# Expert down projection: every other pair of tiles 32 to 119 as seven block products, with sums of blocks on GpSimd

## The chip, the cores and the metric

The kernel runs on one core of one Trainium2 chip. The metric is the device time in microseconds. The profiles name the engines PE (TensorE), PEld (its weight loads), DVE (VectorE), ACT (ScalarE), POOL (GpSimd) and SP (SyncE, which here only issues transfers).

## The reference

Two transformer blocks over 256 tokens of 1024 features, all in float32. The first has two layers, each with a mixer, a feed-forward part with product-key experts, and a gated per-layer embedding. The change is in the last sum of the experts, once for each layer:

```python
def expert_block(args):          # peer_ffn; K = 16 experts for each of 8 heads, of 16384
    xb, eb, gb = args
    ub = jnp.take(u, eb, axis=0)
    act = jax.nn.gelu(jnp.einsum('thkd,td->thk', ub, xb), approximate=False)
    vb = jnp.take(v, eb, axis=0)
    return jnp.einsum('thk,thkd->td', gb * act, vb)
...
x = layer_norm(DN_ALPHA * x + peer_ffn(x, ...), ln_g[i, 1], ln_b[i, 1])
x = x + jax.nn.sigmoid(x @ ple_w_gate[i]) * (p[i] @ ple_w_proj[i])
```

## The kernel before

It gathers no experts. All 16384 are computed for all tokens, as 128 tiles of 128 experts: stage u turns each tile of `u` into a block of gelus [128 experts x 256 tokens], with a gate of zero where a token didn't choose the expert, and these 128 blocks fill `big`. Stage v multiplies block j (as weights of TensorE, in two halves of 128 tokens) with tile j of `v` [128 experts x 1024 features], and adds all 128 into four PSUM banks, `acc`: two token halves by two feature halves of 512. Then the layer norm follows, from `acc` and X.

Each float32 product is made of three in the fp32r type: high x high, low x high and high x low. For a tile of v ScalarE casts the high part from the ring (`take_high`, L433), VectorE subtracts for the low part (`take_low`, L445), and the same two do this for the block of gelus (`stage`, L1574 and L2255, into `x_parts`). TensorE's `split_wide` (L826) then has 3 parts x 2 token halves x 2 feature halves, 12 matmuls of 512 columns. In stage u and in the first tile of most other stages GpSimd makes the low parts (also L445); in stage v it has nothing to do.

The order is written out by hand, one instruction stream for each engine. SP loads tiles into a ring of four (`tile_landed`), each when the low part of the tile four before is done. `w_hi` and `w_lo` have two buffers each: ScalarE casts tile j + 1 once TensorE has begun tile j (`tiles_begun`). `stage(j + 2)` stands behind `take_high(j + 1)`. On all engines the stage is a loop over bodies of eight tiles. Behind the last tile TensorE transposes, runs fillers on zeros (L875) to fill the wait, and takes up the next weight matrix when the layer norm on VectorE, ScalarE and GpSimd is through.

## Time and profile before

| | us |
|---|---|
| median of 3 runs | 2625.51 (2624.88 to 2627.14) |
| profiled execution, its own time | 2623.45 |
| its span, first to last instruction | 2621.7 |
| PE busy | 2583.5 (99%) |
| PEld busy | 2214.6 (84%) |
| DVE busy | 1743.4 (67%) |
| ACT busy | 1495.7 (57%) |
| POOL busy | 670.6 (26%), nearly all of it in the two u stages |

The times of single instructions come from the one profiled execution. A busy TensorE isn't one at its peak, since matmuls are pipelined; how long a tile takes is read from the starts of its matmuls. The idle time of an engine costs nothing by itself: what counts is which wait ends last.

### The profile page before, as it was taken

To read this page: it belongs to the slowest core of one execution; us is meant where nothing else is said; L and a number is where in the kernel's file an instruction comes from. 1 tells how busy PE (TensorE), PEld (TensorE's weight loads), DVE (VectorE), ACT (ScalarE), POOL (GpSimd) and SP (SyncE) were. 2 spreads that over 40 slices of the span, in tenths; PEclk is the share of its full clock that TensorE was granted. 3 is DMA by queue.
4 is the path that set the end of the run, shared out by engine and by line. 5 is a ranking of instruction groups with operands and counts; after the bars stand their busy time and mean duration, and the time that the engine had idled before them with its cause. 6 is when DMAs were issued, how large, how long until landed. Compare 5 with 4: busy or idle time off the path is not lost.

```text
span 2621.7 us, 43906 instructions
## 1 busy us (share of the span) xinstructions
PE 2583.5 (99%) x15010; PEld 2214.6 (84%) x15010; DVE 1743.4 (67%) x3219; ACT 1495.7 (57%) x2852; POOL 670.6 (26%) x310
## 2 busy tenths in 40 slices
PE   8999999999999999999999999999999999999998
PEld 7789988887888887789988887888888887877887
DVE  4568778886555565459778885555567746555774
ACT  4445488885445554444588884444555545564553
POOL 0007877672000000018877671000001000001000
PEclk9999999999999999999999999999999999999999
DMA  6345544445555544345544446555556565535564
GB/s 223 89 160 177 185 156 159 153 156 200 193 192 192 192 162 148 109 153 185 177 156 159 153 162 200 194 193 193 192 169 197 191 194 170 161 111 161 168 192 153
DMA packets 124331, 447.66 MB, mean 171 GB/s; under 512 B 14312, under 2 KB 14952, under 8 KB 123936
## 3 DMA queue, kind: packets, MB, share of 16 engines
q1 hardware_dynamic: 120096, 434.16, 51.0%
q0 software_dynamic: 2608, 9.08, 1.2%
q10 hardware_dynamic: 1488, 2.59, 0.3%
q8 instruction: 83, 1.36, 0.2%
q14 instruction: 56, 0.46, 0.1%
HBM read 444.74 MB, written 1.05 MB: 170 GB/s over the span
## 4 chain that ended last, share of the span: by engine, by line
PE 94%; DVE 2%; ACT 2%; DMA 1%; issue 1%; ACTq 0%; POOL 0%; DVEq 0%
PE ps L826 41%; PE ps L782 21%; PE ps L787 10%; PE ps L798 4%; PE ps L804 4%; PE ps L801 4%; PE ps L1046 3%; PE ps L1118 1%; PE ps L1015 1%; ACT w_hi L433 0%; PE ps L733 0%; DMA ring<-in_v 0%; PE ps L1064 0%; PE ps L887 0%; DVE stats L1937 0%
## 5 line engine op out<-in xcount | busy, mean ns | idle before, releaser
L433 ACT CAST w_hi<-ring 128x1024 fp32r<-128x1024 f32 (+1 forms) x812 | 852.1, 1050 | 765.3 <-PE ps L826 521.2
L445 POOL TENSOR_TENSOR w_lo<-ring,w_hi 128x1024 fp32r<-128x1024 f32 x267 | 641.4, 2403 | 1679.3 <-ACT w_hi L433 1480.7
L445 DVE TENSOR_TENSOR w_lo<-ring,w_hi 128x1024 fp32r<-128x1024 f32 x545 | 664.8, 1220 | 549.8 <-ACT w_hi L433 540.0
L826 PE MATMUL ps<-w_hi,x_parts 128*128 128x512 f32 x2976 | 743.9, 390 | 4.7 <-ACT w_hi L433 3.2
L826 PEld LDWEIGHTS ps<-w_hi,x_parts 128*128 128x128 f32 x2976 | 553.0, 188 | 125.7 <-issue 8.9
L782 PE MATMUL ps<-x_parts,w_hi 128*128 128x512 f32 x2320 | 591.9, 397 | 0.1
L782 PEld LDWEIGHTS ps<-x_parts,w_hi 128*128 128x128 f32 x2320 | 416.0, 189 | 75.5 <-ACT w_hi L433 0.3
L826 PE MATMUL ps<-w_lo,x_parts 128*128 128x512 f32 x1488 | 402.2, 388 | 0.3 <-DVE w_lo L445 0.3
L787 PEld LDWEIGHTS ps<-x_parts,w_lo 128*128 128x128 f32 x2320 | 316.5, 190 | 22.6
L826 PEld LDWEIGHTS ps<-w_lo,x_parts 128*128 128x128 f32 x1488 | 277.8, 188 | 59.4 <-DVE w_lo L445 1.6
L787 PE MATMUL ps<-x_parts,w_lo 128*128 128x256 f32 x2320 | 323.0, 282 | 0.0
L798 PE MATMUL ps<-x_parts,w_hi 128*128 128x256 f32 x784 | 192.8, 284 | 0.0
L801 PE MATMUL ps<-x_parts,w_hi 128*128 128x256 f32 x784 | 192.3, 283 | 0.0
L1394 ACT COPY tops<-ps 128x256 f32<-128x256 f32 x294 | 106.7, 363 | 141.1 <-PE ps L787 137.4
L1542 ACT ACTIVATE SC<-SC 128x128 bf16<-128x128 bf16 x512 | 163.6, 392 | 8.8 <-DVE SC L2207 8.7
L2213 DVE TENSOR_TENSOR SC<-SC,ps 128x512 bf16<-128x512 bf16 x256 | 164.4, 683 | 4.4
L2207 DVE TENSOR_TENSOR SC<-iota,ps 128x1024 bf16<-128x1024 f32 x128 | 154.8, 1209 | 0.1
L798 PEld LDWEIGHTS ps<-x_parts,w_hi 128*128 128x128 f32 x784 | 150.4, 192 | 0.6 <-issue 0.4
L801 PEld LDWEIGHTS ps<-x_parts,w_hi 128*128 128x128 f32 x784 | 150.5, 192 | 0.0
L804 PE MATMUL ps<-x_parts,w_lo 128*128 128x256 f32 x784 | 110.0, 283 | 0.0
L1046 PE MATMUL ps<-SC 128*128 128x128 bf16 x1536 | 108.0, 220 | 0.0
L2255 DVE TENSOR_TENSOR x_parts<-big,x_parts 128x256 fp32r<-128x256 f32 x256 | 106.7, 417 | 0.2
(287 smaller groups left out, 2196.8 us busy)
## 6 DMA issues: line engine op xcount, KB each, us to landing
ring<-in_u SPq DMA_DIRECT2D x256, 512.0 KB, 3.5
ring<-in_v SPq DMA_DIRECT2D x256, 512.0 KB, 4.2
ring<-in_ffn_in SPq DMA_DIRECT2D x88, 512.0 KB, 3.8
ring<-in_ffn_out SPq DMA_DIRECT2D x44, 512.0 KB, 4.2
ring<-in_wq SPq DMA_DIRECT2D x32, 512.0 KB, 3.4
ring<-in_ple_gate SPq DMA_DIRECT2D x16, 512.0 KB, 3.7
SC<-in_rows POOLq DMA_DIRECT2D x11, 512.0 KB, 5.0
ring<-in_a_qk SPq DMA_DIRECT2D x8, 512.0 KB, 4.9
```

What stands on the lines that cost most here:

```text
L433: nc.scalar.copy(part(w_hi, i)[:, used(name)], tile(i)[:, used(name)]).then_inc(tiles_hi, 1)
L445: eng.tensor_tensor(part(w_lo, i)[:, at], tile(i)[:, at], part(w_hi, i)[:, at], ALU.subtract).then_inc(tiles_low[LOW[n][0]], 1)
L782: mm = nc.tensor.matmul(both, hi[:, k, :], x_parts[:, :, k, :], start=(k == 0), stop=False)
L787: mm = nc.tensor.matmul(bank(s)[:, 0:T], lo[:, k, :], x_hi[:, k, :], start=False, stop=(k == KC - 1))
L798: mm = nc.tensor.matmul(bank(s)[:, 0:T], hi[:, k, :], x_hi[:, k, :], start=(k == 0), stop=False)
L801: nc.tensor.matmul(bank(s)[:, 0:T], hi[:, k, :], x_lo[:, k, :], start=False, stop=False)
L804: mm = nc.tensor.matmul(bank(s)[:, 0:T], lo[:, k, :], x_hi[:, k, :], start=False, stop=(k == KC - 1))
L826: mm = nc.tensor.matmul(acc[:, 2 * tb + f, 0:cnt], x[:, k + c, tb * P:(tb + 1) * P], part(w, i)[:, at:at + cnt], start=(first and n == 0 a ...
L1046: mm = nc.tensor.matmul(bank(s)[:, t * P:(t + 1) * P], one_hots[:, n % 2, 1, t], gated_rows[:, n % 2, piece, t], start=(piece == 0), stop= ...
L1542: ins = S.mul(gated_rows[:, n % 2, 2, t], one_hots[:, n % 2, 0, t], gate_low[:, at:at + 1])
L2207: V.tensor_tensor(one_hots[:, n % 2], iota[:, None, None, :].to_broadcast([P, 2, GROUP, P]), chosen[:, :, :, None].to_broadcast([P, 2, GRO ...
L2213: V.tensor_tensor(gated_rows[:, n % 2, piece], one_hots[:, n % 2, 0], part_of[:, :, None].to_broadcast([P, GROUP, P]), ALU.mult).then_inc( ...
```

## The change

In tiles 32 to 119 a body of eight has two mixed pairs, tiles 0 and 1 and tiles 4 and 5 of it, and two pairs of plain tiles as before. A mixed pair is a 2 x 2 block product: rows are the two token halves, columns the two feature halves, and the inner index is the tile of the pair. It is done with seven block products in place of eight (Strassen's scheme in Winograd's form). Three add into `acc` as before. Four add into the banks 4 to 7, over all pairs of the layer, and are folded into X at the end.

What comes with it: GpSimd makes three sums of v's blocks, one more in place, and the low part of the three (`block_sums_of`). ScalarE casts the high part of the sums (`sums_high`). VectorE makes four sums of the gelu blocks (`rows_mixed`) and their low parts (`rows_low`), and ScalarE their high parts. Two blocks of gelus are staged by one instruction (`stage_pair`). Tiles 4 and 5 of a body land in a buffer of their own in `big`, so a pair can stay longer. At the end ScalarE copies the four banks, multiplies X by DN_ALPHA, and GpSimd's `fold` adds them in seven instructions; the layer norm then has the weight 1.0. `ple_side` moves from `big` to `SC` and is copied eight tiles before the mixed ones.

```diff
+            def block_sums_of(layer):                      # GpSimd
+                pool.wait_ge(staged, EXPERT_TILES * layer + 26)
+                def pair(m, b, turns):
...
+                    b21, b22 = tile(i)[:, 0:512], tile(i)[:, 512:D]
+                    b11, b12 = tile(i + 1)[:, 0:512], tile(i + 1)[:, 512:D]
+                    if b or m:
+                        pool.wait_ge(sums_low, turns * MIX_PAIRS + p)
+                    G.tensor_tensor(block_sums[:, 0], b11, b12, ALU.add).then_inc(pair_sums, 1)
+                    made(1)
+                    G.tensor_tensor(block_sums[:, 1], block_sums[:, 0], b22, ALU.add).then_inc(pair_sums, 1)
+                    made(2)
+                    G.tensor_tensor(block_sums[:, 2], block_sums[:, 1], b21, ALU.add).then_inc(pair_sums, 1)
+                    G.tensor_tensor(b12, b12, b22, ALU.add).then_inc(pair_sums, 1)
+                    pool.wait_ge(sums_hi, turns * MIX_PAIRS + (p + 1))
+                    G.tensor_tensor(sum_lo[:], block_sums[:], sum_hi[:], ALU.subtract).then_inc(sums_low, 1)
...
+            def fold(layer):                               # GpSimd, 7 instructions, 4096 elements
+                pool.wait_ge(mix_moved, 5 * layer + 5)
+                G.tensor_tensor(V, m6, m1, ALU.subtract).then_inc(mix_folded, 1)
...
+                def mixed_pair(m, b, turns=0, first=False, last=False):      # TensorE
...
+                    pe.wait_ge(staged, turns * BODY + (EXPERT_TILES * layer + j + 2))
+                    pe.wait_ge(mixed_low, turns * MIX_PAIRS + (p + 1))
+                    def products(group, low, apart):
+                        for n in range(3):
+                            if n == 2 and low:
+                                low()
+                            for dst, x, w in group:
+                                mm = nc.tensor.matmul(dst, x[n % 2], w[n // 2], ...)
+                    own = [ps[:, 4 + n, :] for n in range(4)]
+                    mm = products([(c11, raw(k, one), halves_of(i, left)), (c12, row(3), halves_of(i, right))],
+                                  lambda: lo_here(name, j, turns), lambda dst: False)
+                    begins_tile(mm)
+                    pe.wait_ge(sums_low, turns * MIX_PAIRS + (p + 1))
+                    mm = products([(c21, raw(k, two), sums(2)), (own[1], row(0), sums(0)), (own[2], row(2), sums(1))],
+                                  None, lambda dst: dst is not c21)
+                    begins_tile(mm)
+                    hi_here(name, j + 1, turns)
+                    mm = products([(own[0], raw(k + 1, one), halves_of(i + 1, left)),
+                                   (own[3], row(1), halves_of(i + 1, right))],
+                                  lambda: lo_here(name, j + 1, turns), lambda dst: True)
+                    mm.then_inc(sums_used, 1)
...
+                def sums_high(m, b, turns=0):              # ScalarE
+                    act.wait_ge(pair_sums, turns * (4 * MIX_PAIRS) + (4 * p + 3))
+                    if b or m:
+                        act.wait_ge(sums_used, turns * MIX_PAIRS + p)
+                    S.copy(sum_hi[:], block_sums[:]).then_inc(sums_hi, 1)
+                def mixed_half(s, b, turns=0, last=False):
+                    take_high(act, name, at + s + 1, turns)
+                    stage_pair(at + s + 4, turns)
+                    take_high(act, name, at + s + 2, turns)
+                    if ahead:
+                        sums_high(*where)
+                    take_high(act, name, at + s + 3, turns)
+                    if ahead:
+                        rows_high(*where)
+                    take_high(act, name, at + s + 4, turns)
+                    stage_pair(at + s + 6, turns)
...
+                def mixed_half(s, b, turns=0, last=False): # VectorE
+                    if ahead:
+                        rows_mixed(*where)
+                    take_low(dve, name, at + s + 1, turns)
+                    stage_pair(at + s + 4, turns)
+                    take_low(dve, name, at + s + 2, turns)
+                    take_low(dve, name, at + s + 3, turns)
+                    if ahead:
+                        rows_low(*where)
+                    take_low(dve, name, at + s + 4, turns)
+                    stage_pair(at + s + 6, turns)
...
-                layer_norm(f"v{layer}", f"ln{layer}_1")
+                dve.wait_ge(mix_folded, 7 * (layer + 1))
+                layer_norm(f"v{layer}", f"ln{layer}_1", 1.0)
```

VectorE's loop of the v stage before, from its top, two of the eight tiles (L445 is `take_low`, L2255 is `stage`; REGISTER_ALU and ISA are the loop's arithmetic and waits):

```order
L2260 UNCONDITIONAL_BRANCH
L2260 ISA
L445 TENSOR_TENSOR w_lo<-ring,w_hi 128x1024
L2254 REGISTER_ALU
L2255 ISA
L2255 TENSOR_TENSOR x_parts<-big,x_parts 128x256
L443 REGISTER_ALU
L445 TENSOR_TENSOR w_lo<-ring,w_hi 128x1024
```

The same engine now, in the loop over tiles 32 to 111, the first half of a body without its last two instructions (`big` is also where the row sums and the tiles of the second pair are; L2605 to L2610 is `rows_mixed`, L2616 `rows_low`, L2590 `stage_pair`, L502 `take_low`):

```order
L2605 TENSOR_TENSOR big<-big 128x256
L2601 ISA
L2608 TENSOR_TENSOR big<-big 128x128
L2601 REGISTER_ALU
L2610 ISA
L2610 TENSOR_TENSOR big<-big 128x128
L500 ISA
L502 TENSOR_TENSOR w_lo<-ring,w_hi 128x1024
L2589 REGISTER_ALU
L2590 TENSOR_TENSOR x_parts<-big,x_parts 128x512
L500 REGISTER_ALU
L502 TENSOR_TENSOR w_lo<-ring,w_hi 128x1024
```

Four tiles have ten such instructions on VectorE in place of eight. GpSimd before, between the last low part of stage u and the layer norm's scaling (L445 here is the low part of the next stage's first tile, L669 `scale_first`):

```order
L445 TENSOR_TENSOR w_lo<-ring,w_hi 128x1024 x7
L641 DMA SC<-in_rows 128x1024 x2
L445 TENSOR_TENSOR w_lo<-ring,w_hi 128x1024
L669 TENSOR_TENSOR X<-X,SC 128x512 x2
```

And now, at the same place: the first pair, then (from L813 with `big<-big` on) the second, whose tiles are in `big`:

```order
L773 DMA SC<-in_rows 128x1024 x2
L813 TENSOR_TENSOR big<-ring 128x512
L815 TENSOR_TENSOR big<-big,ring 128x512
L817 TENSOR_TENSOR big<-big,ring 128x512
L818 TENSOR_TENSOR ring<-ring 128x512
L820 TENSOR_TENSOR sum_lo<-big,sum_hi 128x1536
L813 TENSOR_TENSOR big<-big 128x512
L815 TENSOR_TENSOR big<-big 128x512
L817 TENSOR_TENSOR big<-big 128x512
L818 TENSOR_TENSOR big<-big 128x512
L820 TENSOR_TENSOR sum_lo<-big,sum_hi 128x1536
```

A loop with 20 further pairs and the fold follow, all of which read and write SBUF alone.

## Rows read from the trace of the kernel before

**Rows 1.** section 1 of the page, each engine's busy us, share and instructions:

```profile
PE 2583.5 (99%) x15010; PEld 2214.6 (84%) x15010; DVE 1743.4 (67%) x3219; ACT 1495.7 (57%) x2852; POOL 670.6 (26%) x310
```

**Rows 2.** chain that ended last, 600 to 975, start, us, what:

```profile
625.42 341.65 PE ps L826 x1506
967.10 1.23 DVE X L1927
```

**Rows 3.** stretches of both v stages, busy us of each engine (instructions), clock, DMA:

```profile
core 0: us, PE busy (x) PEld busy (x) DVE busy (x) ACT busy (x) POOL busy (x), PEclk, DMA share, GB/s
625.00:967.00 342.00, 341.58 (x1507) 282.87 (x1508) 196.20 (x251) 172.81 (x256) 0.00 (x0) 1.00 0.59 194
1597.00:1937.00 340.00, 340.00 (x1502) 281.52 (x1501) 194.54 (x250) 171.08 (x253) 0.01 (x1) 1.00 0.59 193
```

**Rows 4.** timeline of PE, 955 to 975, start, us, line, operation:

```profile
957.38 1.98 PE L826 MATMUL ps<-w_hi,x_parts 128*128 128x512 f32 x8
...
960.10 1.98 PE L826 MATMUL ps<-w_hi,x_parts 128*128 128x512 f32 x8
...
971.71 1.89 PE L875 MATMUL ps<-zeros 128*128 128x512 bf16 x8
```

**Rows 5.** groups by line, 630 to 950: count, busy us, mean ns, idle:

```profile
L826 PE MATMUL ps<-w_hi,x_parts 128*128 128x512 f32 x942 | 232.8, 389 | 0.0
L445 DVE TENSOR_TENSOR w_lo<-ring,w_hi 128x1024 fp32r<-128x1024 f32 x118 | 144.5, 1225 | 137.0 <-ACT w_hi L433 137.0
L2255 DVE TENSOR_TENSOR x_parts<-big,x_parts 128x256 fp32r<-128x256 f32 x118 | 49.2, 417 | 0.0
L433 ACT CAST w_hi<-ring 128x1024 fp32r<-128x1024 f32 x118 | 124.5, 1055 | 160.9 <-PE ps L826 160.9
L1574 ACT CAST x_parts<-big 128x256 fp32r x118 | 47.6, 403 | 0.0
```

**Rows 6.** waits, 620 to 950: us in total, times, longest:

```profile
ACT w_hi L433 <- PE ps L826: 165.4, 121, 2.8
DVE w_lo L445 <- ACT w_hi L433: 143.7, 120, 3.4
```

**Rows 7.** groups by line, GpSimd, whole span:

```profile
L445 POOL TENSOR_TENSOR w_lo<-ring,w_hi 128x1024 fp32r<-128x1024 f32 x267 | 641.4, 2403 | 1679.3 <-ACT w_hi L433 1480.7 <-DVEq L1833 198.3
L669 POOL TENSOR_TENSOR X<-X,SC 128x512 f32<-128x512 f32 x8 | 10.1, 1270 | 8.2 <-ACT X L1341 8.2
```

**Rows 8.** timeline of DVE and POOL, at 325 and from 602 to 611:

```profile
325.70 0.43 DVE L1814 TENSOR_TENSOR SC<-SC 128x256 f32<-128x256 f32 x1
325.76 2.63 POOL L445 TENSOR_TENSOR w_lo<-ring,w_hi 128x1024 fp32r<-128x1024 f32 x1 [1.15 <-ACT w_hi L433]
...
602.53 2.40 POOL L445 TENSOR_TENSOR w_lo<-ring,w_hi 128x1024 fp32r<-128x1024 f32 x1 [1.13 <-ACT w_hi L433]
...
603.14 0.67 DVE L2223 TENSOR_TENSOR big<-big,ps 128x496 f32<-128x496 f32 x1 [1.88 <-ACT big L1532]
...
605.37 2.41 POOL L445 TENSOR_TENSOR w_lo<-ring,w_hi 128x1024 fp32r<-128x1024 f32 x1 [0.43 <-ACT w_hi L433]
...
605.68 2.38 DVE L2236 TENSOR_TENSOR big<-SC,big 128x256 f32<-128x256 f32 x1 [0.88 <-ACTq L1525]
...
608.16 2.41 POOL L445 TENSOR_TENSOR w_lo<-ring,w_hi 128x1024 fp32r<-128x1024 f32 x1 [0.38 <-ACT w_hi L433]
...
608.92 1.92 DVE L2236 TENSOR_TENSOR big<-SC,big 128x256 f32<-128x256 f32 x1 [0.53 <-ACTq L1525]
```

**Rows 9.** groups by line, VectorE, whole span, L2236 with both operands in SBUF:

```profile
L2236 DVE TENSOR_TENSOR big<-SC,big 128x256 f32<-128x256 f32 x8 | 10.3, 1288 | 4.9 <-ACTq L1525 4.9
```

**Rows 10.** timeline of DVE, the start of the layer norm:

```profile
967.10 1.22 DVE L1927 SCALAR_TENSOR_TENSOR X<-X,ps 128x1024 f32<-128x1024 f32 x1 [1.49 <-PE ps L826]
```

**Rows 11.** section 6 of the page, issue to landing:

```profile
ring<-in_v SPq DMA_DIRECT2D x256, 512.0 KB, 4.2
```

**Rows 12.** stretch where PE is idle most after a v stage:

```profile
972.00:976.00 4.00, 2.64 (x17) 1.71 (x16) 3.32 (x10) 1.15 (x4) 1.50 (x2) 1.00 0.06 23
```

More of the change, by code:

```diff
@@ L430, in take_high @@
             i = TILE[name] + j
[L431 removed]
+            tile_here(act, i, turns)
             part_free(act, i, turns)
@@ L687, in _ @@
                 load_rows(2 * layer + 1, (tiles_gated, tiles_with_gates(layer, EXPERT_TILES - 1)))
+                block_sums_of(layer)
+                fold(layer)
                 take_low(pool, f"ple_gate{layer}", 0)
@@ L1076, in peer, with mixed_body @@
+                def mixed_body(b, turns=0, first=False, last=False):
+                    for s in (0, 4):
+                        if s in MIX_AT:
+                            mixed_pair(MIX_AT.index(s), b, turns, first, last and s == MIX_AT[-1])
+                        for j in range(s + 2 if s in MIX_AT else s, s + 4):
+                            down(MIX_FROM + BODY * b + j, turns)
+                        first = first and MIX_AT[0] > s
                 for j in range(BODY):
                     down(j)
-                with pe.Fori(1, EXPERT_TILES // BODY - 1, 1) as turns:
+                with pe.Fori(1, MIX_FROM // BODY, 1) as turns:
@@ L1079, in peer @@
                     for j in range(BODY, 2 * BODY):
                         down(j, turns - 1)
-                for j in range(EXPERT_TILES - BODY, EXPERT_TILES):
+                moved(pe, SLOT[f"ple_proj{layer}"], 4)
+                mixed_body(0, first=True)
+                with pe.Fori(1, MIX_BODIES - 1, 1) as turns:
+                    mixed_body(1, turns - 1)
+                mixed_body(MIX_BODIES - 1, last=True)
+                for j in range(MIX_TO, EXPERT_TILES):
                     down(j)
+                pe.wait_ge(mix_moved, 5 * layer + 4)
@@ new lines, in mixed_half @@
+                def mixed_half(s, b, turns=0, last=False):
+                    at, name = MIX_FROM + BODY * b, f"v{layer}"
+                    n = (s + 4) % BODY
+                    ahead = n in MIX_AT and not last
+                    where = (MIX_AT.index(n), b + (s + 4) // BODY, turns) if ahead else None
+                    if s in MIX_AT:
+                        third_sum(at + s + 1, b, turns)
+                    take_high(act, name, at + s + 1, turns)
[8 more added lines that the diff above has]
+                    stage_pair(at + s + 6, turns)
@@ new lines, in rows_low @@
+                def rows_low(m, b, turns=0):
+                    p = pairs_before(layer, b, m)
+                    dve.wait_ge(mixed_hi, turns * MIX_PAIRS + (p + 1))
+                    V.tensor_tensor(row_lo[:], row_sums[:], row_hi[:], ALU.subtract).then_inc(mixed_low, 1)
+                def mixed_half(s, b, turns=0, last=False):
+                    at, name = MIX_FROM + BODY * b, f"v{layer}"
+                    n = (s + 4) % BODY
+                    ahead = n in MIX_AT and not last
+                    where = (MIX_AT.index(n), b + (s + 4) // BODY, turns) if ahead else None
+                    if ahead:
[8 more added lines that the diff above has]
+                    stage_pair(at + s + 6, turns)
```

266 lines of the change are left out of this document (245 added, 21 removed).

## The prediction, made before the changed kernel ran

> **What bounds the kernel now.** I read the engines' shares first, then the chain that ended last, then the stage that is changed, and last every place where GpSimd and VectorE work at once. TensorE is busy for 99% of the span [rows 1]; the reader should take from it that all other engines have slack on average, GpSimd most. The chain of waits says the same of the changed stage: one unbroken piece of 341.65 us of L826 matmuls, from 625.42 on, and then VectorE's layer norm [rows 2]. Both layers have the stage, with 1508 and 1502 matmuls in 342 and 340 us, at a granted clock of 1.00, with VectorE at 57% and GpSimd at zero [rows 3]. In the timeline a tile takes 2.72 us, 12 matmuls of 512 columns, so 0.2267 us each [rows 4]; four tiles take 10.88. VectorE does 1.225 + 0.417 us in a tile and ScalarE 1.055 + 0.403 [rows 5], and each waits for the engine ahead of it, ScalarE 165.4 us for TensorE and VectorE 143.7 us for ScalarE in 330 us [rows 6]. So today TensorE is the bound, and a matmul removed there is worth 0.2267 us as long as nothing else grows beyond it.
>
> **What it removes.** 88 tiles of a layer (32 to 119) become 22 mixed pairs and 22 pairs of plain tiles. A pair was 24 matmuls and is now 7 products of 3 parts, 21. Their width stays 512 and each has its own weight load as before. Four tiles (one mixed pair, two plain tiles: a half body) go from 48 matmuls to 45: 10.20 us in place of 10.88, and 44 times 0.68 is 29.9 us in the two layers. That is all that can be won.
>
> **What it adds, for four tiles.** On GpSimd, where nothing ran: four tensor_tensor of 512 elements and one of 1536. Rows give 2.40 us for 1024 and 1.27 for 512 [rows 7], so 2.21 ns an element and 0.14 us fixed; the five are 4 x 1.27 + 3.53 = 8.61 us, of which 3584 x 2.21 ns = 7.92 is the work on elements. On VectorE: four low parts of 1024 (as before), two stagings of 512 in place of four of 256, and for the row sums 256, 128, 128 and then 512: 6144 elements. By 1.225 for 1024 and 0.417 for 256 [rows 5] it is 1.05 ns an element and 0.15 fixed: 6.45 us on elements, and with the ten fixed parts 7.9. ScalarE gets two casts of 512, 0.62 each, for four of 256, a cast of 1536 (1.49) and one more of 512: 4.2 + 1.2 + 1.5 + 0.6 = 7.5 us. Taken one engine at a time all of this lies beside 10.2 us of matmuls and costs nothing.
>
> **Where the cover is gone.** The engines cannot be taken one at a time. At 605.68 VectorE begins a tensor_tensor of 256 elements from SC and big, both in SBUF. It ought to take 0.42 us and takes 2.38, while GpSimd's own subtraction runs from 605.37 to 607.78; VectorE's ends at 608.06, 0.28 us after, which is the 0.27 that 256 elements need. The next pair of rows repeats it: 1.92 us, ending 0.27 after GpSimd's. It goes the other way too: GpSimd's at 325.76 takes 2.63 us and ends 2.26 after VectorE's two-SBUF-operand instruction, which is 1024 elements of 2.21 ns. An instruction of VectorE with one operand in PSUM, at 603.14, lies wholly inside GpSimd's 602.53 to 604.93 and takes its usual 0.67 [rows 8]. So two SBUF operands on VectorE and a tensor_tensor on GpSimd exclude each other for the whole instruction, in either order, with only the fixed part hidden. In the kernel before this costs next to nothing, since in the stages where GpSimd splits tiles VectorE mostly reads PSUM. In the changed stage every instruction of both engines has only SBUF operands.
>
> The Trainium skill (SBUF — State Buffer, "Who interferes with whom") says the same of two SBUF inputs and a GpSimd instruction that reads SBUF, and calls it an exclusive lock for the whole instruction. The rows agree, though each shows one instruction held up, none both engines queued without a break. By that rule the two engines' work adds up, as it does below; were the port shared without loss, the 10.2 us of the matmuls would stand.
>
> The floor for four tiles is then 7.92 + 6.45 = 14.4 us. The ceiling is all durations end to end, 8.6 + 7.9 = 16.5, with about 1 us in which both wait for someone else: 17.5. Both lie above 10.2. To choose I lay one half body out, from t = 0 where TensorE ends the mixed pair. ScalarE's cast of 1536 waits for that and ends at 1.55. GpSimd's 1536 then holds the port from 1.63 to 5.16. The low part of the second plain tile has its high part at 2.6 and must wait: it ends at 6.24, where TensorE wanted it at 4.53, and TensorE is through with that tile at 7.2 in place of 5.4. From 5.2 on GpSimd's four 512s (1.13 each) and VectorE's low rows 0.54, low part 1.08, staging 0.54 take turns: 13.0. The row sums, three with a wait of each other, bring 13.95, the next low part 15.1, and two last matmuls end the pair at 15.6. TensorE waits in four pieces of 0.8 to 1.8 us. I take 15.6; the order of the turns moves it by 0.6 down or 1 up. There are 21 such half bodies in a layer, since the last prepares no pair and only gains 0.68: 21 x (15.6 - 10.88) - 0.7 = 98.4 us a layer, 196.9 for both. At the floor it is 21 x 3.5 - 0.7 = 73 a layer, at the ceiling 138.
>
> **The way in and out.** For the first pair GpSimd begins once tile 26 is staged, with some 16 us ahead, and its 7.9 us beside four tiles of VectorE's fit. I take 1 us a layer, between 0 and 3. At the end ScalarE copies four banks and scales X beside tiles 121 to 124: a cast (1.05), a copy of 512 (0.59) and 2048 elements (1.92) behind the start of tile 123, so the fold on GpSimd begins about 1.0 us after tile 124 does. Its seven instructions hold 4096 elements, 9.05 us, with some 1.1 of fixed parts and waits in a chain, and VectorE's three last low parts take 3 x 1.08 of the port: 14.4 after the start of tile 124. VectorE waits for it ahead of the layer norm, which before began 9.7 us after that tile's start (967.10 against 957.38) [rows 4, 10]. The layer norm is wholly on the path there, TensorE has only a transposition and fillers beside it. So 5 us a layer, between 1 and 8. The bank copies moved, ple_side's new place and the 10 more semaphores I take at nothing: ScalarE has 3 us to spare in four tiles. Transfers too: a tile lands in 4.2 us [rows 11], its number is unchanged, and pair tiles are asked for eight ahead. If that cover went, a half body that waits for a landing would cost what is left of it, within the ceiling.
>
> **Sum.** Profiled execution before 2623.45; + 196.9 + 2 + 10 = 2832.4. The median of the runs shown is 2.06 over the profiled one, so 2834 us.
>
> **Rivals.**
> A, the other side, not slower: the port is not held when both queues are full (or the two long stalls were something else), and everything added hides behind TensorE. Then 2623.45 - 29.9 + 2 + 10 = 2605.6, and 2607.6 by the median. For it: the engines' shares, and that such stalls are rare: L2236 has eight instructions with both operands in SBUF, at a mean of 1288 ns against some 420 [rows 9]. Against it: stretches that end to 0.01 us with the other engine's instruction, both ways, in both layers. It decides if the union of both engines' work comes below 10.2 us in four tiles. 5%.
> B: TensorE's idle pieces, a third of the stage, cost it its clock. A matmul at the lower level of 1.2 GHz would take up to twice as long, 45 x 0.453 = 20.4 us for four tiles, TensorE bound again: 21 x 9.5 = 200 a layer, 3037 us if it held all through. Against it: in the slice of before where TensorE is idle most, 972 to 976 with 2.64 of 4 us busy, the granted clock is 1.00 [rows 12]; no row here has it at the lower level. The Trainium skill (TensorE: Matmul & The Clock Gate, Part 1) has the clock depend on how busy the engine has been lately; by it part of the stage could fall, by the row none. 5%.
> C: the turns go badly. If VectorE always loses to GpSimd's four 512s, or the 1536 waits behind the low parts and the pair waits for it, a half body passes the ceiling, at 18.5 say: 21 x 7.6 x 2 = 320, 2956 us. For it: the sum_lo, the low part and the row sums are each on the way to TensorE, with one buffer each. 7%.
> D: the lock is there, but VectorE's short instructions slip in unseen, so that a half body is 12 to 14 us: around 2725. Nothing in the rows speaks for it. 4%.
>
> **How the numbers follow.** The forecast has 79%. Its own range runs from the floor, 2625.5 + 146 + 2, to the ceiling, 2625.5 + 276 + 22: 2774 to 2924. I give 2772 to 2930; that leaves out A, B, most of C and D, and little of the forecast. A measurement of this kernel tells about 0.2%, 5 us. Faster: A and a bit of doubt, 0.06; within 0.2%: 0.01; slower: 0.93.
>
> **What would show it.** Right: in the changed stage TensorE at about 65% busy, four tiles every 15 to 16 us, waits of L1299 and the plain tiles' matmuls for VectorE's low parts, low parts of 1024 that last up to 4.6 us where GpSimd's 1536 lies beside them, GpSimd's 512s stretched from 1.27 towards 2.3, a clock still at 1.00, and a layer norm that waits for GpSimd. Wrong: VectorE's low parts at 1.22 throughout and four tiles in 10.2 (A); a stage clock near half (B); TensorE waiting mostly for landings.

## The result, and the profile after

| | before | after |
|---|---|---|
| median, us | 2626.26 (4 runs, 2624.88 to 2627.14) | 2837.77 (4 runs, 2837.3 to 2840.0) |
| profiled execution's own time | 2623.45 | 2840.0 |
| its span | 2621.7 | 2837.3 |

The ratio is 1.0808, with an interval of 1.0794 to 1.0823: 211.5 us slower, where 2834 us and a range of 2772 to 2930 were predicted. The span grew by 215.6 us.

Section 1 and three groups of section 5 of the page of after (busy us, mean ns of one, idle time before):

```profile
PE 2637.0 (93%) x14869; PEld 2212.5 (78%) x14878; DVE 2100.4 (74%) x3301; ACT 1579.8 (56%) x2856; POOL 1190.8 (42%) x544
...
L502 DVE TENSOR_TENSOR w_lo<-ring,w_hi 128x1024 fp32r<-128x1024 f32 (+1 forms) x501 | 688.8, 1379 | 383.4 <-ACT w_hi L490 372.9
...
L820 POOL TENSOR_TENSOR sum_lo<-big,sum_hi 128x1536 fp32r<-128x1536 f32 x44 | 171.4, 3895 | 94.9 <-ACT sum_hi L1847 94.9
...
L2590 DVE TENSOR_TENSOR x_parts<-big,x_parts 128x512 fp32r<-128x512 f32 x94 | 183.7, 1955 | 0.0
```

By the code TensorE has 132 matmuls fewer, 3 for each of 44 pairs, and the weight loads show just that (15010 and 14878; nine matmul records are missing from the trace). Its busy share falls from 99% [rows 1] to 93%. VectorE's staging of 512 elements, 0.69 us by the prediction's figures (512 x 1.05 ns and 0.15), lasts 1.96 in the mean, and GpSimd's low part of 1536, 3.53 by them, lasts 3.90. The windows of after answer to [rows 3]; this one is the inside of both changed stages:

```profile
750.00:1020.00 270.00, 211.52 (x813) 156.48 (x812) 261.43 (x180) 129.45 (x144) 205.42 (x90) 0.95 0.41 139
1830.00:2080.00 250.00, 196.00 (x751) 144.59 (x749) 242.44 (x167) 120.01 (x134) 188.35 (x82) 0.95 0.42 140
```

VectorE is busy for 261.43 of 270 us. Nearly half of that is waiting inside instructions, since an instruction that is held up counts as busy: 270 us hold 17.8 times four tiles, and by the prediction's 7.9 us each VectorE's own work is 141 us. Without the other engine's rows this looks like an engine at its limit. The groups of 750 to 1030 show it against [rows 5] and [rows 7]:

```profile
L502 DVE TENSOR_TENSOR w_lo<-ring,w_hi 128x1024 fp32r<-128x1024 f32 x57 | 101.3, 1790 | 3.9 <-ACT w_hi L490 3.9
L1019 PE MATMUL ps<-w_hi,x_parts 128*128 128x512 f32 x293 | 80.8, 421 | 0.0
L2590 DVE TENSOR_TENSOR x_parts<-big,x_parts 128x512 fp32r<-128x512 f32 x38 | 79.7, 2097 | 0.0
L820 POOL TENSOR_TENSOR sum_lo<-big,sum_hi 128x1536 fp32r<-128x1536 f32 x18 | 71.7, 3983 | 41.9 <-ACT sum_hi L1847 41.9
...
L813 POOL TENSOR_TENSOR big<-big 128x512 f32<-128x512 f32 x9 | 18.8, 2087 | 8.2 <-DMA big<-in_v 7.5 <-POOL sum_lo L820 0.7
```

The low part takes 1790 ns where it took 1225, and GpSimd's first sum 2087 where such an instruction took 1270. The waits of the same stretch (us in total, times, longest) say who paid:

```profile
PE ps L1019 <- DVE w_lo L502: 31.9, 18, 2.5
PE ps L1299 <- DVE w_lo L502: 24.1, 29, 1.3
```

Then half a body in the timeline of after (start, us; in brackets the idle time before and what ended it):

```profile
802.50 4.38 POOL L820 TENSOR_TENSOR sum_lo<-big,sum_hi 128x1536 fp32r<-128x1536 f32 x1 [2.90 <-ACT sum_hi L1847]
...
803.91 4.05 DVE L502 TENSOR_TENSOR w_lo<-ring,w_hi 128x1024 fp32r<-128x1024 f32 x1 [0.40 <-ACT w_hi L490]
...
807.05 2.06 POOL L813 TENSOR_TENSOR big<-big 128x512 f32<-128x512 f32 x1 [0.17 <-POOL sum_lo L820]
807.89 1.77 DVE L2616 TENSOR_TENSOR row_lo<-big,row_hi 128x512 fp32r<-128x512 f32 x1
808.02 1.19 PE L1019 MATMUL ps<-w_lo,x_parts 128*128 128x512 f32 x4 [0.91 <-DVE w_lo L502]
...
809.71 0.50 PE L1299 MATMUL ps<-w_hi,x_parts 128*128 128x512 f32 x1 [0.50 <-DVE row_lo L2616]
...
811.94 0.50 PE L1299 MATMUL ps<-w_lo,x_parts 128*128 128x512 f32 x1 [1.04 <-DVE w_lo L502]
...
816.97 0.50 PE L1299 MATMUL ps<-w_lo,x_parts 128*128 128x512 f32 x1 [1.33 <-DVE w_lo L502]
```

The low part of 803.91 ends at 807.96, 1.08 us behind GpSimd's end at 806.88, and 1.08 is what its 1024 elements need. GpSimd's sum ends at 809.11 and VectorE's row_lo 0.55 later, which is 512 elements. TensorE waits 0.91 + 0.50 + 1.04 + 1.33 = 3.78 us in this half body. A body takes 30.27 us (for example 802.56 to 832.83), or 15.13 for four tiles, against 10.88 before. TensorE needs 10.20 of them at full clock.

The other half of this body has one longer wait, and a stretch in which TensorE runs slower. The two halves as windows, and lines of TensorE in the second:

```profile
802.56:817.70 15.14, 11.36 (x46) 8.14 (x46) 14.56 (x10) 7.23 (x8) 13.00 (x6) 1.00 0.37 139
817.70:832.83 15.13, 12.42 (x46) 9.46 (x46) 14.77 (x12) 7.14 (x8) 10.01 (x6) 0.89 0.42 139
```

```profile
822.01 1.41 PE L1019 MATMUL ps<-w_lo,x_parts 128*128 128x512 f32 x4 [2.46 <-DVE w_lo L502]
823.22 3.40 PE L1019 MATMUL ps<-w_hi,x_parts 128*128 128x512 f32 x8
```

One instruction of VectorE, the first row sum (`rows_mixed`), in three half bodies in a row:

```profile
798.36 1.51 DVE L2605 TENSOR_TENSOR big<-big 128x256 f32 x1
...
813.50 1.51 DVE L2605 TENSOR_TENSOR big<-big 128x256 f32 x1
...
828.63 1.51 DVE L2605 TENSOR_TENSOR big<-big 128x256 f32 x1
```

In the first half the granted clock is 1.00, in the second 0.89, where eight matmuls last 3.40 us in place of 1.98, and still both take 15.1 us (TensorE's first plain matmuls behind a pair start at 802.40, 817.54 and 832.66). VectorE's instruction comes every 15.10 to 15.15 us from 738 to 1025, while TensorE begins its pairs 12.6 to 17.7 us apart. So the pace of the stage is that of VectorE and GpSimd taking turns, and a slower TensorE only fills some of its own waits.

**The ledger.** Landmarks of the two traces (starts of the same tiles), us added:

| | predicted, a layer | layer 0 | layer 1 |
|---|---|---|---|
| way in (start of tile 30 to first pair, less 5.44) | 1 | 7.6 | 8.3 |
| 22 half bodies (239.4 before) | 98.4 | 329.1 - 239.4 = 89.7 | 332.4 - 239.4 = 93.0 |
| fold: start of tile 124 to layer norm (9.72 before) | 5 | 14.03 - 9.72 = 4.3 | 4.3 |
| behind the layer norm's start (to tile 30 of layer 1; to the end) | 0 | 3.3 | 2.7 |

They sum to 213.3. The other 2.4 us of the span's 215.6 lie ahead of tile 30 of layer 0, nearly all within the first 140 us, where both kernels do the same.

### The profile page after: what moved, and what is told of

Same layout as the page of the kernel before. It is cut to its first block, busy times and chain, and to the rows that moved or that the text cites. A ratio compares the mean times of both kernels' runs of the same rounds, so it can differ in the third digit from the quotient of the medians.

```text
span 2837.3 us, 44061 instructions
## 1 busy us (share of the span) xinstructions
PE 2637.0 (93%) x14869; PEld 2212.5 (78%) x14878; DVE 2100.4 (74%) x3301; ACT 1579.8 (56%) x2856; POOL 1190.8 (42%) x544
## 3 DMA queue, kind: packets, MB, share of 16 engines
HBM read 444.74 MB, written 1.05 MB: 157 GB/s over the span
## 4 chain that ended last, share of the span: by engine, by line
PE 73%; DVE 14%; issue 6%; ACT 3%; POOL 2%; DMA 1%; DVEq 1%; ACTq 0%; SPq 0%; POOLq 0%
PE ps L1019 23%; PE ps L975 19%; PE ps L980 10%; DVE x_parts L2590 4%; DVE w_lo L502 3%; PE ps L991 3%; PE ps L997 3%; PE ps L994 3%; PE ps L1239 3%; DVE big L2605 2%; DVE row_lo L2616 2%; PE ps L1299 1%; ACT w_hi L490 1%; DMA ring<-in_v 1%; PE ps L1376 1%
## 5 line engine op out<-in xcount | busy, mean ns | idle before, releaser
L490 ACT CAST w_hi<-ring 128x1024 fp32r<-128x1024 f32 x768 | 804.9, 1048 | 699.9 <-PE ps L1019 377.6
L502 POOL TENSOR_TENSOR w_lo<-ring,w_hi 128x1024 fp32r<-128x1024 f32 x267 | 641.3, 2402 | 983.4 <-ACT w_hi L490 784.8
L502 DVE TENSOR_TENSOR w_lo<-ring,w_hi 128x1024 fp32r<-128x1024 f32 (+1 forms) x501 | 688.8, 1379 | 383.4 <-ACT w_hi L490 372.9
L1019 PE MATMUL ps<-w_hi,x_parts 128*128 128x512 f32 x2272 | 597.3, 404 | 23.6 <-ACT w_hi L490 21.1
L1019 PEld LDWEIGHTS ps<-w_hi,x_parts 128*128 128x128 f32 x2272 | 438.5, 196 | 126.7 <-issue 17.3
L1019 PE MATMUL ps<-w_lo,x_parts 128*128 128x512 f32 x1136 | 323.0, 402 | 72.5 <-DVE w_lo L502 72.2
L980 PE MATMUL ps<-x_parts,w_lo 128*128 128x256 f32 x2320 | 323.0, 282 | 0.0
L1019 PEld LDWEIGHTS ps<-w_lo,x_parts 128*128 128x128 f32 x1136 | 214.2, 193 | 137.2 <-DVE w_lo L502 94.0
L820 POOL TENSOR_TENSOR sum_lo<-big,sum_hi 128x1536 fp32r<-128x1536 f32 x44 | 171.4, 3895 | 94.9 <-ACT sum_hi L1847 94.9
L2590 DVE TENSOR_TENSOR x_parts<-big,x_parts 128x512 fp32r<-128x512 f32 x94 | 183.7, 1955 | 0.0
L813 POOL TENSOR_TENSOR big<-ring 128x512 f32<-128x512 f32 x22 | 44.4, 2017 | 190.6 <-DMA ring<-in_v 189.8
```

The lines of the kernel that those rows point to most:

```text
L490: nc.scalar.copy(part(w_hi, i)[:, used(name)], tile(i)[:, used(name)]).then_inc(tiles_hi, 1)
L502: eng.tensor_tensor(part(w_lo, i)[:, at], tile(i)[:, at], part(w_hi, i)[:, at], ALU.subtract).then_inc(tiles_low[LOW[n][0]], 1)
L820: G.tensor_tensor(sum_lo[:], block_sums[:], sum_hi[:], ALU.subtract).then_inc(sums_low, 1)
L980: mm = nc.tensor.matmul(bank(s)[:, 0:T], lo[:, k, :], x_hi[:, k, :], start=False, stop=(k == KC - 1))
L1019: mm = nc.tensor.matmul(acc[:, 2 * tb + f, 0:cnt], x[:, k + c, tb * P:(tb + 1) * P], part(w, i)[:, at:at + cnt], start=(first and n == 0 a ...
L2590: V.tensor_tensor(x_lo[:, j % BODY:j % BODY + 2, :].rearrange("p a b -> p (a b)"), pair_rows(j, turns), x_hi[:, j % BODY:j % BODY + 2, :]. ...
```

## The experiments

In what follows "the port" is what VectorE, with two SBUF operands, and a GpSimd that reads SBUF cannot use at once; the traces show the turns, not the wiring. "The kernel before" ran beside each, with medians of 2625.0 to 2626.3. The first two, and two later ones, put work on GpSimd beside the unchanged stage of before. Where a range is given a kernel ran four times (one_pair_spread eleven times), where it isn't, once. Ahead of tile 30 of layer 0, where no edit reaches, the profiled executions differ by up to 3.7 us, so a difference of a few us from a single execution is only as good as the stretch of the trace that shows it.

### reads_beside_1024

```diff
+ # kernel before; GpSimd, once for each of the tiles 0 to 119 of v
+ pool.wait_ge(staged, ...)
+ nc.gpsimd.tensor_tensor(tops [128 x 1024], iota, ident, ALU.add)
```

> The kernel before, and one GpSimd tensor_tensor of 1024 elements (both operands constants in SBUF, the result unused) beside each of tiles 0 to 119 of both v stages. Nothing waits for it but the layer norm. Theory, the port is held for whole instructions: VectorE needs 1280 x 1.05 ns = 1.34 us a tile and GpSimd 1024 x 2.21 ns = 2.26, together 3.6 to 3.9 in place of 2.72, so 240 tiles x 0.9 to 1.2 = 215 to 285 us more, about 2860; VectorE's low parts last up to 3.5 us, TensorE waits for them. Rival, the long instructions after the change come from its own chains of waits: nothing waits here, so the time stays 2626 within 5 us and the low parts at 1.22.

Measured: 2849.37 us. Groups of 640 to 960 of this run:

```profile
L693 POOL TENSOR_TENSOR tops<-iota,ident 128x1024 f32<-128x1024 f32 x88 | 291.4, 3311 | 31.9 <-DVE x_parts L2270 31.9
L2270 DVE TENSOR_TENSOR x_parts<-big,x_parts 128x256 fp32r<-128x256 f32 x88 | 230.0, 2614 | 0.0
L841 PE MATMUL ps<-w_hi,x_parts 128*128 128x512 f32 x699 | 184.0, 405 | 57.3 <-DVE x_parts L2270 57.3
```

A tile takes 3.67 us. The elements of both engines, 1024 x 2.21 ns and 1280 x 1.05 ns, are 3.61. Nothing of the tile's own work changed, so 224 us come from one instruction on an engine that was idle. It was the staging that stretched to 2.61 us, not the low part (1211 ns), since GpSimd's instruction starts ahead of it each time.

### writes_beside_1024

```diff
- nc.gpsimd.tensor_tensor(tops [128 x 1024], iota, ident, ALU.add)
+ nc.gpsimd.tensor_tensor(tiny [128 x 1], iota, ident, ALU.add)
+ nc.gpsimd.memset(tops [128 x 1024], 0.0)
```

> The same place and number, but a GpSimd memset of 1024 elements, which reads no SBUF, behind a tensor_tensor of one element that carries the wait. Theory, only GpSimd's reads meet VectorE's second SBUF operand: 2626 within 5 us, low parts at 1.22 us for all tiles. Rival, any GpSimd instruction holds the port: low parts stretched by what the memset lasts, up to as slow as with the reads if it lasts as long.

Measured: 2622.95 us. Groups of 640 to 950:

```profile
L448 DVE TENSOR_TENSOR w_lo<-ring,w_hi 128x1024 fp32r<-128x1024 f32 x114 | 139.6, 1225 | 132.3 <-ACT w_hi L436 132.3
...
L694 POOL MEMSET tops<- 128x1024 f32 x112 | 106.8, 954 | 0.0
```

Writing alone holds nobody up: VectorE's low part stays at 1225 ns. The memset is shorter than the sum (0.95 us against 2.40), so this run also has less GpSimd work beside the tiles; sums_as_writes fills the time instead.

### sums_as_writes

It leaves out the block sums: from the second body on GpSimd writes zeros to a free buffer at the places of its five sums, with the same semaphores.

```diff
+ if b:
+     for n in range(4):                  # for each sum of 512
+         G.memset(tops[:, 0:1024], 0.0).then_inc(pair_sums, 1)
+     pool.wait_ge(sums_hi, ...)
+     for n in range(3):                  # for the low part of 1536
+         ins = G.memset(tops[:, 0:1024], 0.0)
+     ins.then_inc(sums_low, 1)
+     return
```

> The changed kernel; from the second body of each layer on GpSimd's four sums and the low part of the sums are replaced by memsets of 1024 elements (one for each sum, three for the low part) on a free buffer, all waits between the engines kept. It leaves the block sums of those pairs out. Theory, the port: with no reads four tiles take TensorE's 10.2 us in place of 15.13, 42 x 4.9 = 207 us less, about 2632; what is left over 2626 is the way in, the fold and the layer norm. Rival, the chain through GpSimd and ScalarE (sums, cast, low part, one buffer each) sets the pace: the memsets keep the chain, so the time stays above 2750 as far as they last as long.

Measured: 2640.77 us (2638.38 to 2644.07), ratio 1.0056 (1.0038 to 1.0074). Four tiles take 10.20 us to the hundredth (half bodies start at 802.76, 812.96 and so on), with GpSimd busy for 47.5 of 51 us. So the waits, the buffers, the casts, the landings and the four more accumulators of the mixed body cost nothing by themselves. The reads of SBUF by GpSimd are what costs. The 15 us that stay above before are in the parts that this run kept. By the landmarks of the ledger its span is 19.3 us longer: the way in 15.6, the fold 8.6, behind the layer norms 6.9 and ahead of tile 30 of layer 0 3.0, less 14.9 that the 44 half bodies save, the first body with its real sums among them.

### sums_on_vector

```diff
- block_sums_of(layer)                    # GpSimd
+ sums_of_blocks(*where)                  # VectorE: the same four sums
+ sums_lower(*where)                      # and the low part, then rows_mixed
```

> The changed kernel with all five GpSimd instructions of a pair on VectorE, and ScalarE's cast of the sums one place later; the fold stays on GpSimd. Theory, the port: VectorE now has 9728 elements x 1.05 = 10.2 us and 15 fixed parts of 0.07 to 0.15, 11.3 to 12.5 us in four tiles, for 15.13 when the two take turns: 42 x 2.6 to 3.8 = 110 to 160 us less, 2680 to 2730, though the busiest engine gets 4 us more work. It stays over the 2626 of before. Rival, VectorE was full by its own work (it shows 97% busy in the stage): with more of it the time rises over 2838.

Measured: 2683.52 us (2682.08 to 2684.73), ratio 1.022 (1.0202 to 1.0239). Groups of 750 to 980:

```profile
L502 DVE TENSOR_TENSOR w_lo<-ring,w_hi 128x1024 fp32r<-128x1024 f32 x60 | 73.0, 1217 | 6.9 <-ACT w_hi L490 6.9
L2634 DVE TENSOR_TENSOR sum_lo<-big,sum_hi 128x1536 fp32r<-128x1536 f32 x18 | 31.5, 1749 | 0.0
```

VectorE is the bound now, at 46.1 of 47.1 us, 11.77 for four tiles. Still this is 154 us faster than the change itself: on VectorE an element of a sum takes 1.05 ns of the shared way into SBUF, on GpSimd 2.21. The sums are better piled on the engine that is full than given to the one that is idle.

### one_pair_gpsimd

```diff
-MIX_AT = (0, 4)
+MIX_AT = (0,)          # one mixed pair in a body of eight
-MIX_FROM, MIX_TO = 32, 120
+MIX_FROM, MIX_TO = 32, 112
-                    if n == 5:
+                    if n == 6:
                         sums_high(0, 0)
```

> The changed kernel with one mixed pair in a body of eight (tiles 0 and 1 of it, from tile 32 to 111), sums on GpSimd as in the change; the mixed tiles end at 112, so that the fold lies beside plain tiles, and the first cast of the sums comes one tile later. Theory, the port: in eight tiles GpSimd holds it 7.9 us and VectorE 11.8, 19.7 together, under TensorE's 21.1 (93 matmuls), so the pace is no longer the port's. But the one long instruction of 3.4 us can still come ahead of a low part that has some 1.7 us to spare: a body takes 21.1 to 22.8 us, for 21.76 of plain tiles, and the time is 2615 to 2670. Rival, the pace after the change is set by a chain of waits a pair and not by the sum of the port's use: a pair would still cost its 4.9 us, 20 x 4.9 = 98 us over, about 2710.

Measured: 2728.86 us (2722.86 to 2729.6), ratio 1.0389 (1.0371 to 1.0406). This missed: the elements of eight tiles need 19.7 us of the port at 21.08 us of matmuls, and most bodies take 26.8. The rival's figure, 2710, was nearer, and so was its price: a pair costs about 5 us over plain tiles. Timeline:

```profile
838.22 3.81 POOL L820 TENSOR_TENSOR sum_lo<-big,sum_hi 128x1536 fp32r<-128x1536 f32 x1 [1.26 <-ACT sum_hi L1847]
838.60 3.99 DVE L2590 TENSOR_TENSOR x_parts<-big,x_parts 128x512 fp32r<-128x512 f32 x1
...
842.51 2.35 DVE L502 TENSOR_TENSOR w_lo<-ring,w_hi 128x1024 fp32r<-128x1024 f32 x2
843.78 1.20 PE L1019 MATMUL ps<-w_lo,x_parts 128*128 128x512 f32 x4 [2.03 <-DVE w_lo L502]
...
844.81 3.34 PE L1019 MATMUL ps<-w_hi,x_parts 128*128 128x512 f32 x8
```

One sum_lo holds the staging for 3.3 us, and behind the staging stand the low parts of two tiles, one of which TensorE wants at 841.75. Eight matmuls then take 3.34 us in place of 1.98, in a stretch with a granted clock of 0.79. Two bodies of layer 0 with a granted clock of 1.00 throughout take 25.1 and 25.2 us (770.47 to 795.58 is one), so of the 5.7 us over 21.08 some 1.6 are the clock and 4.1 the waits. An average over the body hid this: GpSimd's five instructions run from 830.29 to 842.03, within less than half of the 26.8 us, since the first waits each time for the pair's tiles to land (117.2 us in eight waits). SP asks for them only when the low parts of the pair before are done (at 825.12). So the rival is right in part: here a chain of landing, sums, cast and low part sets where the holds fall, and what a hold costs is the low part behind it. For the change itself that is ruled out, since its half bodies keep 15.13 us and sums_as_writes, with the same chain and GpSimd busy for 93% of it, 10.20.

### one_pair_vector

```diff
 # one_pair_gpsimd with the sums on VectorE as in sums_on_vector, but
+                    # those of the next pair already in this body
+ if s == 0 and b + 1 < MIX_BODIES:
+     sums_of_blocks(0, b + 1, turns)     # VectorE, beside the plain tiles
```

> As one_pair_gpsimd, but the five instructions of the sums on VectorE, the four sums in the half body ahead of the low part; GpSimd has only the fold. Theory, the port: nothing contends; VectorE has some 17 us of work in eight tiles for 21.1 of TensorE, so a body takes 21.1 us: 20 x 0.68 = 13.6 us less than before, with 1 to 3 us a layer for the way in: 2614 to 2620, the fastest of all. Rival, mixed pairs cost TensorE something of their own (its seven products wait more than plain tiles do): at or over 2626.

Measured: 2652.22 us (2648.03 to 2652.74), ratio 1.0099 (1.0082 to 1.0116). A miss too: the body takes 22.43 us in place of 21.1. Four block sums and three row sums in a row on VectorE (816.09 to 819.92) stand ahead of one low part:

```profile
819.84 1.22 DVE L502 TENSOR_TENSOR w_lo<-ring,w_hi 128x1024 fp32r<-128x1024 f32 x1
...
821.11 1.19 PE L1018 MATMUL ps<-w_lo,x_parts 128*128 128x512 f32 x4 [0.87 <-DVE w_lo L502]
```

### one_pair_spread

```diff
 # one_pair_vector, with the next tile's low part ahead of the row sums,
 # and the first pair's sums begun a tile earlier
+ take_low(dve, name, at + s + 1, turns)
+ if j == MIX_FROM - 3:
+     sums_of_blocks(0, 0)
```

> one_pair_vector with VectorE's order mended: the row sums behind the first low part of the half body (six instructions in a row held that low part up, TensorE waited 0.87 us for it in each body), the first pair's sums three tiles earlier, and the first cast behind that of tile 32. Theory, in a kernel without GpSimd's reads only such single late low parts cost anything: a body falls from 22.4 to between 21.1 and 21.5 us and the way in to 1 us: 2612 to 2622, under the 2625 of before. Rival, mixed pairs have a cost on TensorE beyond their matmuls: a body stays at 22 us or more, 2635 to 2650.

Measured: 2630.57 us (2628.36 to 2634.97), ratio 1.0019 (1.001 to 1.0028), against 2626.13 of before. (The first pair's sums come one tile earlier, not three as the expectation says.) The body is as expected, 21.27 us against 21.76 of eight plain tiles, and the window 720 to 950 has TensorE busy for 229.85 of 230 us:

```profile
720.00:950.00 230.00, 229.85 (x1007) 186.45 (x1006) 183.70 (x210) 131.73 (x153) 11.37 (x6) 1.00 0.60 193
```

That gains 10 x 0.49 = 4.9 us a layer. The way in and the longer first body take 3.7 us of it back in layer 0 (waits of 1.87 us for a high part and 1.18 for sum_lo among them) and 5.9 in layer 1, and tiles 112 to 124, beside the fold, another 2.3 a layer (34.9 us in place of 32.6). The total missed; no version tried here is faster than the kernel before.

### reads_beside_512 and reads_beside_1536

```diff
 # reads_beside_1024 with another size
+ nc.gpsimd.tensor_tensor(tops [128 x 512], ...)   # beside each tile
+ nc.gpsimd.tensor_tensor(SC [128 x 1536], ...)    # beside each fourth tile
```

> The kernel before with a GpSimd tensor_tensor of 512 elements beside each of tiles 0 to 119. The port is then in use 1.34 + 1.13 = 2.5 of 2.72 us. Theory, what counts is how late one low part comes: it has 1.7 us to spare and the instruction holds the port 1.13, so no change, 2622 to 2630. Rival, contention costs in proportion to GpSimd's reads: half of the 224 us of reads_beside_1024, 2737.

> The kernel before with a GpSimd tensor_tensor of 1536 elements beside every fourth tile of 0 to 119: fewer elements than in reads_beside_512 (384 a tile for 512), the port in use 2.2 of 2.72 us on average. Theory, the length of one hold counts: 3.4 us is more than a low part has to spare, so 60 times a low part is 0.4 to 1.7 us late: 25 to 100 us more, 2650 to 2725, most of it nearer 2660. Rival, the average use of the port counts: no change, 2626.

Measured: 2625.87 and 2672.11 us. By elements the first holds the port for 1.13 + 1.34 of 2.72 us, 91%, and the second for 3.39 + 5.38 of 10.88, 81%. The one that uses more of it costs nothing, the other 46 us. A group and a wait of the first, in 640 to 950:

```profile
L693 POOL TENSOR_TENSOR tops<-iota,ident 128x512 f32<-128x512 f32 x114 | 268.7, 2357 | 41.4 <-DVE x_parts L2270 41.4
L2270 DVE TENSOR_TENSOR x_parts<-big,x_parts 128x256 fp32r<-128x256 f32 x115 | 173.9, 1512 | 0.0
...
L448 DVE TENSOR_TENSOR w_lo<-ring,w_hi 128x1024 fp32r<-128x1024 f32 x114 | 139.6, 1225 | 6.3
```

and of the second:

```profile
L448 DVE TENSOR_TENSOR w_lo<-ring,w_hi 128x1024 fp32r<-128x1024 f32 x106 | 193.6, 1827 | 84.5 <-ACT w_hi L436 84.5
L841 PE MATMUL ps<-w_lo,x_parts 128*128 128x512 f32 x424 | 116.9, 398 | 12.3 <-DVE w_lo L448 12.3
```

VectorE has slack behind each cast (it waited 1.16 us a tile for one before), and a hold of 1.13 us fits into it: the staging stretches, the low part is in time. A hold of 3.4 us doesn't, and TensorE waits in each fourth tile.

### cast_later

```diff
-                    if n == 5:
-                        sums_high(0, 0)
...
+                sums_high(0, 0)          # behind the high part of tile 32
```

> The changed kernel; only ScalarE's first cast of the block sums of a layer is moved behind the casts of tiles 31 and 32. After the change TensorE waits 4.65 us for tile 31's high part, which stands behind this cast, and runs its eight matmuls at the lower clock. Theory, the order on ScalarE makes this: the wait goes, TensorE begins the first pair about 5 us earlier and waits then for the low part of the sums: 4 to 6 us less a layer, 2826 to 2831. Rival, the late landing of tile 33 sets it, whatever the order: no change, 2838.

Measured: 2832.63 us, 5 below the median of after. What happens in after on the way in (timeline):

```profile
701.48 14.13 SPq L689 DMA_DIRECT2D ring<-in_v  x3
...
705.15 1.29 POOL L813 TENSOR_TENSOR big<-ring 128x512 f32<-128x512 f32 x1 [84.59 <-DMA ring<-in_v]
...
709.17 1.47 ACT L1847 CAST sum_hi<-big 128x1536 fp32r<-128x1536 f32 x1 [5.95 <-POOL big L817]
710.54 1.04 ACT L490 CAST w_hi<-ring 128x1024 fp32r<-128x1024 f32 x1
710.72 3.46 POOL L820 TENSOR_TENSOR sum_lo<-big,sum_hi 128x1536 fp32r<-128x1536 f32 x1 [0.36 <-ACT sum_hi L1847]
...
711.62 3.64 DVE L502 TENSOR_TENSOR w_lo<-ring,w_hi 128x1024 fp32r<-128x1024 f32 x1 [5.03 <-ACT w_hi L490]
711.64 3.78 PE L1019 MATMUL ps<-w_hi,x_parts 128*128 128x512 f32 x8 [4.65 <-ACT w_hi L490]
```

ScalarE's cast of the sums stands ahead of tile 31's high part and waits 5.95 us for GpSimd, which waited for tile 33 to land. That tile goes to the ring of four, so SP asks for it at 701.48, when the low part of tile 29 is done, and GpSimd begins 3.7 us later. TensorE waits 4.65 us, and its eight matmuls then take 3.78 in place of 1.98, at a granted clock of 0.50. With the cast moved behind, the first pair starts 8.3 us after tile 30 in place of 13.0, but TensorE waits in it for row_lo (2.71) and a low part (3.14). From tile 30 to tile 120 layer 0 takes 339.4 us for 342.1 in after, so 2.7 are won. Layer 1 takes 342.6 for 346.2, but more_fillers, which leaves this order alone, takes 342.6 there too. Another 1.6 us of the difference lie ahead of tile 30. So about 3 us are shown to come from the order, less than the 4 to 6 a layer expected.

### more_fillers

```diff
-... "ln0_1": 8, ... "ln1_1": 8 ...
+... "ln0_1": 22, ... "ln1_1": 22 ...     # matmuls on zeros while the layer norm runs
```

> The changed kernel with 22 in place of 8 matmuls on zeros (0.22 us each) at the turn of each layer's second layer norm. After the change TensorE idles 3.2 us there and its next 24 transposes take 5.49 us where they took 2.94. Theory, the idle time that the fold makes costs the clock: with the fillers the granted clock stays at 1.00 and the transposes take 2.9 to 3.1 us, 2.5 us less a layer, 2833. Rival, the transposes wait for data: no change.

Measured: 2830.07 us, 7.7 below the median of after. The timeline of after, then of this run:

```profile
1072.02 1.67 PE L1068 MATMUL ps<-zeros 128*128 128x512 bf16 x7
...
1076.90 1.16 PE L1080 MATMUL ps<-tops,X 128*128 128x128 f32 x8 [3.21 <-DVE tops L2250]
...
1079.84 5.49 PE L1080 MATMUL ps<-tops,X 128*128 128x128 f32 x24 [1.78 <-DVE tops L2250]
```

```profile
1071.68 4.91 PE L1068 MATMUL ps<-zeros 128*128 128x512 bf16 x22
...
1079.73 2.94 PE L1080 MATMUL ps<-tops,X 128*128 128x128 f32 x24 [1.79 <-DVE tops L2250]
```

In after the layer norm starts 2.6 us behind TensorE's last product, since it waits for the fold. The fillers are over too early, TensorE idles for 3.21 us, the granted clock is 0.50 in 1080 to 1084, and 24 transpositions take 5.49 us. With fillers through the gap they take 2.94, as before, and the granted clock is 1.00 from 1068 to 1084. By the landmarks of the ledger 3.3 us are back behind the layer norm of layer 0 and 2.1 behind that of layer 1, 5.4 in all. The rest of the 7.7 isn't the fillers': the half bodies of layer 1 took 3.0 us less in this execution.

### mixed_until_112

```diff
-MIX_FROM, MIX_TO = 32, 120
+MIX_FROM, MIX_TO = 32, 112
-                    if n in (0, 2):
+                    if n % 2 == 0 and MIX_TO + 4 + n < EXPERT_TILES:
```

> The changed kernel with the mixed tiles ending at 112 in place of 120, so that the copies, X's scaling and the fold lie beside tiles 113 to 122 and are over before the last tile. Theory, the fold ahead of the layer norm costs 4.3 us a layer and the idle time behind it 3.2 more by the clock; a body of mixed tiles costs 30.3 where plain ones take 21.8: 2 x (8.5 + 7.5) = 32 us less, 2806. Rival, the fold's instructions delay as many low parts there as they saved at the end: only the 17 us of the bodies, 2821.

Measured: 2808.47 us, 29.3 below after, near the 32 expected. Two half bodies a layer become plain, which by the ledger is worth 2 x 2 x (15.2 - 10.88) = 17 us, and the rest, 12, is the fold and what came behind it: with the fold beside plain tiles the transpositions take 2.94 us again. The fold isn't free there, as the rival had it: tiles 112 to 124 take 34.9 us in place of 32.6.

## Why the prediction was right, and where it was not

**The lock, and with it the main term: right.** "Two SBUF operands on VectorE and a tensor_tensor on GpSimd exclude each other for the whole instruction" was read from four pairs of single rows [rows 8]. reads_beside_1024 shows it with both engines queued in every tile; writes_beside_1024 and sums_as_writes show that it is the reads, since GpSimd full of writes leaves four tiles at 10.20 us. The Trainium skill (SBUF — State Buffer, "Who interferes with whom") says that a GpSimd instruction that only writes does not contend with two SBUF inputs of VectorE; the runs agree, with low parts at 1225 ns beside memsets of 954. Rival A and rival D are out.

**The half body: right in mechanism, 0.3 to 0.5 us too high.** The hand layout gave 15.6. The stage gives (329.1 - 10.2) / 21 = 15.2 in layer 0 and 15.3 in layer 1, and 15.13 in its steady part. The pieces held in part: one half of the body has four waits of 0.5 to 1.3 us, predicted as 0.8 to 1.8, the other mainly one of 2.46. The 14.4 us of the elements are nearly reached, so by this reckoning the port is in use for 95% of the time. Summed over both layers the term was 196.9 and is 182.7.

**The way in: wrong, 2 us against 15.9.** I let GpSimd begin at tile 26 and gave it 16 us, with the pair's tiles "asked for eight ahead". Tile 33 is in the ring of four and is asked for only when the low part of tile 29 is done. So GpSimd began at 705.15, 4.4 us before the pair would have started at the pace of before (704.10, the start of tile 30, and 5.44), and ScalarE's queue passed the delay on to tile 31's high part. The working had a wait in it whose releaser is a landing, and priced it as if the data were there. cast_later gives 2.7 of layer 0's 7.6 us to the order of the casts. That the other 4.9 are all due to the late landing was not tested.

**The fold: 4.3 for 5, and something behind it for nothing.** Its 14.4 us are 14.03. What I missed is that a late layer norm leaves TensorE with nothing, and that this costs clock: 2.7 to 3.3 us a layer. more_fillers confirms it, with 5.4 of these 6.0 us back.

**"A clock still at 1.00": wrong, at no cost in the steady stage.** The stage has 0.95, a mean of stretches at the full 2.4 GHz and some at 1.2, and the matmuls of a plain tile last 421 ns in the mean in place of 389. But the half body with 1.00 throughout takes as long as the one with 0.89. The first holds 3.78 us of waits and 10.20 of work at full clock. The remaining 1.15 are not the clock: behind each wait the second matmul starts 0.33 us after the first in place of 0.227, and a matmul is counted busy for 0.39 us, some 0.17 beyond the start that the next would have had, about 1.1 us for four waits. Rival B had the sign of the clock right, and its cost only where TensorE is what the rest waits for, on the way in and behind the layer norm. I had taken the clock from one slice of 4 us with 1.4 us idle [rows 12], and there it had held. The Trainium skill (TensorE: Matmul & The Clock Gate, Part 1) has the clock follow what the engine has lately done; the trace agrees, with 0.50 behind an idle 3.21 us and 1.00 where fillers closed that gap.

The total came within 4 us since the half bodies, 14 us too high, offset the way in, 14 too low. That part is luck, and so is a smaller one: the fold's 1.4 us too many against 6.0 behind the layer norms that the sum did not have.

**What stays open.** The first 140 us of the profiled execution of after are 2.4 us longer, though the code there is the same. It isn't the change: reads_beside_512, built on the kernel before, begins stage v as much later (621.00 for 618.56), and from 112 to 126 both have a mean granted clock of 0.76, where the execution of before has 0.88. Why some executions are granted less there is open. Not tried was a fold or way in for one_pair_spread that costs nothing tried, which would have to leave about 10 us of 2626 to win.

## What to carry to other kernels

Before work is moved to GpSimd beside a VectorE that reads two SBUF operands, add up both engines' elements as one resource (here 2.21 and 1.05 ns each), and then ask of each single instruction how long it holds, and what is queued behind the one it holds up: 512 elements beside every tile were free at 91% of the port, 1536 beside every fourth cost 46 us at 81%. Where such sums must be made, the engine that is already full but quicker with an element (2683.5 us) can beat the idle one (2838). Where a queue hands a wait on, price it from the landing that ends it, and give TensorE something to do in a gap of 3 us.
